# Seven-product groups and stored weight parts in the second half of a two-layer hybrid encoder

## The reference

```
for l in range(2):
    h = rmsnorm(x, norm_gain[l])
    q, k, v, g_attn, x_rnn, g_rnn = split(h @ w_in[l])       # 2048 x 4352
    attn = sliding window attention with sinks and rotary positions (16 heads, 2 kv heads, head size 64)
    rnn  = RG-LRU(causal width-4 conv(x_rnn)), run as a scan over the tokens
    x = x + concat(attn * silu(g_attn), rnn * silu(g_rnn)) @ w_out[l]   # 2048 x 2048
out = rmsnorm(x, final_gain)
```

## Time and profile before

| | |
|---|---|
| time, median of 3 runs | 2304.1 us (2302.57 to 2304.14) |
| time of the profiled execution | 2304.23 us |
| its span | 2301.7 us |
| PE busy | 2292.8 us, 100% of the span |
| DVE busy | 1565.0 us, 68% |
| ACT busy | 1339.1 us, 58% |
| granted clock of PE | 1.00 |
| DMA, mean over the span | 125 GB/s |

### The profile page before, as it was taken

One profiled execution on the slowest core, in us unless ns is written; L12 is line 12 of the kernel. 1 busy time (PEld: TensorE's weight loads), 2 busy tenths in 40 slices (PEclk: granted clock), 3 DMA queues, 4 the chain that ended last, 5 costly groups with the idle time before them and its releaser, 6 DMA issues.

```text
span 2301.7 us, 36298 instructions
## 1 busy us (share of the span) xinstructions
PE 2292.8 (100%) x13798; PEld 1919.3 (83%) x13798; DVE 1565.0 (68%) x2546; ACT 1339.1 (58%) x2564; POOL 32.3 (1%) x58
## 2 busy tenths in 40 slices
PE   9999999999999999999999999999999999999999
PEld 8877888899888888889888888888988888888898
DVE  7658868656646877856675786885565478778555
ACT  7557666445546857645564676763455557666444
POOL 1110000000000000000000000000000000000000
PEclk9999999999999999999999999999999999999999
DMA  8886334545333233344534333344543333333444
GB/s 259 237 243 174 88 92 120 152 138 139 96 93 98 86 89 92 96 145 139 163 110 152 111 95 89 96 139 138 142 131 96 97 91 86 93 92 96 117 136 152
DMA packets 141389, 287.48 MB, mean 125 GB/s; under 512 B 16416, under 2 KB 20768, under 8 KB 138784
## 3 DMA queue, kind: packets, MB, share of 16 engines
q1 hardware_dynamic: 138096, 259.91, 38.1%
q0 software_dynamic: 2688, 25.17, 4.5%
q10 hardware_dynamic: 432, 0.10, 0.0%
HBM read 276.73 MB, written 33.55 MB: 135 GB/s over the span
## 4 chain that ended last, share of the span: by engine, by line
PE 96%; DVE 2%; DMA 1%; ACT 1%; issue 0%; DVEq 0%; POOL 0%; ACTq 0%; POOLq 0%
PE proj L682 80%; PE proj L703 10%; PE ps_at L811 2%; DMA wall<-in_w 1%; PE ps_at L786 1%; PE ps_at L830 1%; PE proj L722 1%; ACT wcut L905 0%; DVE wcut L1307 0%; PE proj L749 0%; PE ps_at L640 0%; DVE mixed L1791 0%; DVE acc L1402 0%; ACT operand L942 0%; PE ps_at L764 0%
## 5 line engine op out<-in xcount | busy, mean ns | idle before, releaser
L682 PE MATMUL proj<-operand,wcut 128*128 128x512 f32 x8376 | 1944.0, 391 | 1.3 <-DVE xr L1558 1.3
L682 PEld LDWEIGHTS proj<-operand,wcut 128*128 128x128 f32 x8376 | 1563.7, 188 | 337.9 <-issue 10.3
L1307 DVE TENSOR_TENSOR wcut<-wall,wcut 128x512 fp32r<-128x512 f32 x871 | 600.1, 689 | 582.0 <-ACT wcut L905 575.1
L905 ACT ACTIVATE wcut<-wall 128x512 fp32r<-128x512 f32 x870 | 548.3, 630 | 547.2 <-DMA wall<-in_w 381.0
L703 PE MATMUL proj<-xsum_out,wcut 128*128 128x256 f32 x1104 | 136.8, 283 | 0.0
L703 PEld LDWEIGHTS proj<-xsum_out,wcut 128*128 128x128 f32 x1104 | 134.9, 192 | 0.6
L703 PEld LDWEIGHTS proj<-operand,wcut 128*128 128x128 f32 x828 | 105.3, 191 | 3.9 <-DVE proj L1371 0.3
L703 PE MATMUL proj<-operand,wcut 128*128 128x256 f32 x828 | 106.6, 283 | 0.0
L1011 ACT ACTIVATE gy<-proj 32x512 f32<-32x512 f32 x144 | 85.1, 591 | 26.6 <-PE proj L682 22.1
L1102 ACT ACTIVATE sqr<-ps_at,pars 64x512 f32<-64x512 f32 x64 | 43.9, 685 | 91.8 <-PE ps_at L830 91.4
L1063 ACT ACTIVATE prob<-ps_at,stat 128x128 f32<-128x128 f32 x256 | 90.1, 363 | 0.8
(11 more groups left out here) (173 smaller groups left out, 1520.6 us busy)
## 6 DMA issues: line engine op xcount, KB each, us to landing
wall<-in_w SPq DMA_DIRECT2D x710, 256.0 KB, 2.6
wall<-weight_sums SPq DMA_DIRECT2D x92, 256.0 KB, 2.7
weight_sums<-in_blocks POOLq DMA_DIRECT2D x36, 512.0 KB, 6.5
wall<-in_blocks SPq DMA_DIRECT2D x69, 256.0 KB, 2.6
x<-in_xt SPq DMA_DIRECT2D x16, 512.0 KB, 3.8
mixed<-in_xt SPq DMA_DIRECT2D x14, 512.0 KB, 6.7
weight_sums<-weight_sums POOLq DMA_DIRECT2D x12, 512.0 KB, 5.2
gw<-in_gates SPq DMA_DIRECT2D x32, 128.0 KB, 2.6
```

The costliest lines, as they stand in the source:

```text
L682: last = pe.matmul(bank_of(l, 2 * g + m)[:, :], wcut[:, n % RING, a, c:c + P], operand[:, k, b, :], start=(i == 0 and k == 0), stop=(k == ...
L905: act.activation(wcut[:, u % RING, 0, :], wall[:, u % RING, 1, :], ACT.Copy).then_inc(w_hi, 1)
L1307: dve.tensor_tensor(wcut[:, u % RING, 1, :], wall[:, u % RING, 1, :], wcut[:, u % RING, 0, :].bitcast(F32), ALU.subtract).then_inc(w_lo, 1)
```

## The change

The groups 7 to 16 of layer 1 and 4 to 16 of layer 2 of the in-projection are computed in seven products too, in the second half only. For it:

- the first half computes the same groups with eight full-width units, four of them on blocks (`beats_of`, kind "block"); after a unit's weights are split, both parts (512 KB) are stored to a new DRAM tensor `cuts`, for seven of the eight units of each group (`STORED`, 161 in all);
- the second half loads such a unit's two parts ready-made (`READY`, 161 units of 512 KB); ACT and DVE have no split to make for them, and PE waits for the load itself;
- the sums of blocks of these groups are built by POOL in 12 more batches, at times given by `OPENS`: five batches at once, four more from (half 1, layer 2) slot 1, six from (half 2, layer 1) slot 4, the last three from (half 2, layer 2) slot 1;
- in the second half `operand_sums` runs for the in-projection at the slots of `T_AT` (already in the code); its space is that of x, so in (half 2, layer 2) x is stored (4 MB, slots 1 to 4) and reloaded;
- in the second half a group's second query tile is moved out one slot after the first instead of four, and `rope` waits for the shifted copy before both of its multiplications;
- `IN_LAST` becomes 16, by which x is reloaded eight slots later.

```diff
-IN_LAST = 15
-IN_SEVEN = {(0, 0): (), (0, 1): (), (1, 0): (), (1, 1): ()}
+IN_LAST = 16
+IN_SEVEN = {(0, 0): (), (0, 1): (), (1, 0): range(7, IN_LAST + 1), (1, 1): range(4, IN_LAST + 1)}
...
-CUT_AT, READY, STORED = {}, set(), []
-SPLIT_NO = {n: n + 1 for n in range(TOTAL + UPG - RING)}
+KEYS = []
+CUT_AT = {}
+for n, (h, l, kind, g, j) in enumerate(UNIT):
+    if h == 0 and zone_of(g) == "in" and g in BUILT[l] and (kind, j) != ("block", WHOLE[A21]):
+        CUT_AT[key_of(l, kind, g, j)] = n
+        KEYS.append(key_of(l, kind, g, j))
+READY = {n for n, (h, l, *unit) in enumerate(UNIT) if h > 0 and key_of(l, *unit) in CUT_AT}
+STORED = sorted(CUT_AT.values())
+SPLIT = [n for n in range(TOTAL + UPG - RING) if n not in READY]
+SPLIT_NO = {n: i + 1 for i, n in enumerate(SPLIT)}
...
+def stores_through(n):
+
+    return sum(m % RING == n % RING for m in STORED if m <= n)
...
-Q_AT = [2 * UPG + 4 * t for t in range(AT)]
+Q_AT = [[2 * UPG + UPG * (t // 2) + (4, 1)[h] * (t % 2) for t in range(AT)] for h in range(HALVES)]
...
+OPENS = {5: (0, 1, 1), 9: (1, 0, 4), 15: (1, 1, 1)}
...
+                if n in READY:
+                    from_n = CUT_AT[key_of(l, kind, g, j)]
+                    sp_.wait_ge(cut_out[from_n % RING], 16 * stores_through(from_n))
+                    sp_.dma_start(wcut[:, n % RING, :, :].rearrange("p a c -> p (a c)").bitcast(F32),
+                                  cuts[KEYS.index(key_of(l, kind, g, j))]).then_inc(w_in[n % RING], 16)
+                    return
                 sp_.dma_start(wall[:, n % RING, 1, :], source(at)).then_inc(w_in[n % RING], 16)
...
                                 sp_.wait_ge(unit_done, u + 1)
+                                if u in STORED:
+                                    sp_.wait_ge(cut_out[u % RING], 16 * stores_through(u))
                                 w_load(u + RING)
+                            if u + 2 in STORED:
+
+                                sp_.wait_ge(w_lo, SPLIT_NO[u + 2])
+                                sp_.dma_start(cuts[KEYS.index(key_of(l, *UNIT[u + 2][2:]))],
+                                              wcut[:, (u + 2) % RING, :, :].rearrange("p a c -> p (a c)").bitcast(F32)
+                                              ).then_inc(cut_out[(u + 2) % RING], 16)
...
+                if n in OPENS:
+                    pool.wait_ge(built[S4], 32 * n - 16)
+                    add(S4, n - 1, A12)
+                    pool.wait_ge(unit_done, at_unit(*OPENS[n]))
...
-                if before:
+                if before and n not in OPENS:
...
-                pe.wait_ge(w_lo, SPLIT_NO[n])
+                if n in READY:
+                    pe.wait_ge(w_in[n % RING], 16 * (n // RING + 1))
+                else:
+                    pe.wait_ge(w_lo, SPLIT_NO[n])
...
             def rope(h, l, n, tile):
 
+                dve.wait_ge(shift_done, per_layer(h, l, 4 * (AT + 1), 4 * n + 4))
                 dve.tensor_tensor(gy[:, 0, :], bank_of(l, tile)[:, :], tab[:, 0, :], ALU.mult)
-
-                dve.wait_ge(shift_done, per_layer(h, l, 4 * (AT + 1), 4 * n + 4))
```

More of the change, by code:

```diff
@@ L294, in build @@
         x_kept = nc.dram_tensor("x_kept", (4, P, KT // 4 * TOK), F32).ap()
+        cuts = nc.dram_tensor("weight_cuts", (len(KEYS), P, 2 * KU * GW), F32).ap()
         rout = mu
@@ L320, in build @@
         built = {n: sem(f"built{n}") for n in SUMS}
+        cut_out = [sem(f"cut_out{i}") for i in range(RING)]
         kept = [sem(f"kept{i}") for i in range(4)]
@@ L1210, in _ @@
                             key_cross(h, l)
-                        if s in Q_AT:
-                            t = Q_AT.index(s)
+                        if s in Q_AT[h]:
+                            t = Q_AT[h].index(s)
                             shift(h, l, t + 1, tile_of("q", t))
@@ L1744, in _ @@
                         for t in range(AT):
-                            if s == Q_AT[t] + 1:
+                            if s == Q_AT[h][t] + 1:
                                 query(h, l, t)
```

## The result

| | before | changed |
|---|---|---|
| time, median | 2304.12 us (2302.57 to 2304.82, 4 runs) | 2330.1 us (2326.29 to 2333.69, 4 runs) |
| span of the profiled execution | 2301.7 us | 2328.5 us |
| PE busy | 2292.8 us | 2286.7 us |
| mean granted clock of PE | 1.000 | 0.995 |

The account below looks back on a forecast made before the run. The prediction took PE to bound the kernel: 2304.23 us, less 17.7 gained, plus 1 (queries), 0.5 (gates, inputs, `lead_sums`) and 2, 2, 1 (POOL's overlaps), gives 2293.0 us. Its range was 2286 to 2303 us.

Parts of the forecast that it names:

- What bounds the kernel: Whole kernel: PE, busy 2292.8 of 2301.7 us; only fewer PE units or PE waits can move the time.
- the gain: Second half: 23 groups turned into seven products save 0.77 us each, 17.7 us in all, the ceiling.
- POOL's overlaps: Four places where POOL's batches run beside new stores or loads, (A) to (D): 0, 2, 2 and 1 us.
- (B): First half, layer 2: batches 5 to 8 beside stores from near 652 us; 2 us lost (0 to 8).
- (C): Second half, layer 1: six batches beside ready-made loads from near 1285 us; 2 us lost (0 to 8).
- (D): Second half, layer 2: x stored in slots 1 to 4 beside three batches; 1 us lost (0 to 6).
- (A): Start of the run: batches 0 to 4 end near 175 us, stores begin near 163; 12 us of overlap, hidden.
- the query tiles: Second half: second tile out after 8.3 of 11.0 us, in time except the last query group; 1 us lost.
- The last pair of layer 2: Second half, layer 2, slots 40 to 42: exponents and normalisation queue ahead, late by 0 to 2 us; 1 taken.
- gates, inputs and `lead_sums`: New groups of the second half: small margins before PE needs them; 0.5 us lost (0 to 5).
- the second rival: Late evacuation: PE waits for DVE in every new group, gain gone, 2304 us (band 2299.7 to 2308.7); chance 0.11.
- The third rival: Stores and loads don't fit the DMA, SP falls behind in every stored group: 2333 us; chance 0.10.

Follow-up runs that it names:

- e9: Changed kernel with ten new groups in each layer, old query slots, POOL's batches apart from stores, last layer's x stored and summed later: 2290.96 us, ratio 0.995.
- e2: Changed kernel with the same eighteen POOL batches started elsewhere, mostly beside out-projection groups: 2339.92 us, ratio 1.0163.
- e3: Changed kernel with only the last three POOL batches moved, to (half 2, layer 1) slot 144: 2329.93 us, ratio 1.0101.
- e1: Changed kernel without POOL's twelve new batches, in-projection groups reading out-projection sums instead: 2313.85 us, ratio 1.0046.
- e12: e9 with the five batches of (half 1, layer 2) begun at slot 54, where stores begin, instead of slot 1: 2338.1 us, ratio 1.0151.
- e5: Changed kernel with POOL's copies and adds cut into pieces of 2 KB instead of 32 KB and 8 KB: 2341.81 us, ratio 1.0162.
- e6: Changed kernel with the query tiles of (half 2, layer 1) back at their old slots: 2321.98 us, ratio 1.0085.
- e8: Changed kernel with POOL's pieces of 2 KB and old query slots in (half 2, layer 1) and for layer 2's first pair: 2327.61 us, ratio 1.0107.

## Why the prediction was wrong

**What bounds the kernel** and **the gain** were right: 23 groups in seven products give 20.7 us, I had 17.7. The pace of 21.00 us holds where no attention runs; where scores and values run a new group gains some 0.95 us instead of the 0.77 I took, which I have not explained.

**Failed: POOL's overlaps were under-sized, 5 us for 28.** The places (B), (C), (D) were named, and (A) was rightly nothing. B: predicted 2 (0 to 8), measured 10.4. C: 2 (0 to 8), measured 3.2 beside the output stores and 6.2 beside the ready-made loads. D: 1 (0 to 6), measured 8.2. The sum of shares of 1.33, 16 us of work too much, pointed the right way. The error was to call 10 us of it hidden and to discount the rest by the row in which PE lost only 1.6 us from 28 to 204 us: there SP asked for a share of 0.3 and the sum stayed under 1.

I also read the parts' beginnings 8 us too soon from the earlier trace rows: the first matmul of (half 1, layer 2) starts at 578.8 us in the kernel before, that of (half 2, layer 1) at 1148.5. That left B's overlap as long as I had it; at C POOL worked from 1174 to some 1363 us and ready-made loads began at 1307.5, 55 us of overlap instead of 40.

The runs give a price for each place. Beside plain loads (shares 0.33 + 0.56) a batch costs 0 to 0.3 us (before, e9). Beside seven-product groups of the out-projection (0.49 + 0.56) it costs 1.4 to 3 us (e2, e3), which the shorter time of six units may explain as well. Beside stores (0.73 + 0.56) it costs 5 to 9 us (changed kernel, e1, e12).

That POOL would keep its share when SP asks for more I had as the consequence of a rule of the Trainium skill ("DMA: Bandwidth & Descriptors", Queues, rings and completion order). At the full queue of e12 the trace agrees with that consequence, 52.6%. That the size of the packets is the reason is not shown: in e5 POOL kept 53.4% with pieces of 2 KB, at queues not quite full. I gave it 8 us at B; the chain of the changed kernel shows why it is more, a store landing late, then the load that had to wait for it on SP:

```profile
672.02 14.02 DMA weight_cuts<-wcut
...
686.11 4.95 DMA wall<-in_blocks
...
691.15 0.64 ACT wcut L942
...
694.62 9.47 DMA weight_cuts<-wcut
...
706.19 10.05 DMA wall<-in_w
...
722.19 3.02 PE proj L719 x12
```

I had allowed a store 4 us and 10 us of lateness to be hidden once. The two on the chain took 14.0 and 9.5, and SP's wait for a store delays everything behind it: 32.6 us of such waits between 655 and 720 us, the longest 8.0. By itself such a wait costs nothing: e9 has 111.5 us of them in the whole run, none over 2.8.

**Failed: the query tiles, 1 us for 18.** I worked out when the second tile is out of its bank (8.3 us), and asked only whether that is in time for PE. I did not name what is queued behind ACT's wait, which is the weight splits that PE needs next. ACT (waits in brackets), then PE, around slot 41 of (half 2, layer 1):

```profile
1282.94 0.64 ACT L942 ACTIVATE wcut<-wall 128x512 fp32r<-128x512 f32 x1
1290.12 2.43 ACT L1048 ACTIVATE gy<-proj 32x512 f32<-32x512 f32 x4 [6.54 <-DVE q L1532]
...
1293.96 0.64 ACT L942 ACTIVATE wcut<-wall 128x512 fp32r<-128x512 f32 x1
```
```profile
1294.14 1.98 PE L823 MATMUL ps_at<-kboth,q 64*64 64x128 f32 x32 [5.03 <-ACT prob L1100]
1296.05 4.35 PE L719 MATMUL proj<-operand,wcut 128*128 128x512 f32 x12
1301.78 13.89 PE L719 MATMUL proj<-operand,wcut 128*128 128x512 f32 x60 [1.37 <-DVE wcut L1344]
```

Eleven microseconds pass between two splits, with a new unit due every 2.72. DVE's query stands behind a weight split that waits for ACT, and behind an operand sum; ACT's next shift waits for that query. And in layer 1, where the first new group is 7, nobody needs those banks sooner; e6, e8 and e9 do without. The last pair of layer 2, which I priced at 1 us (0 to 2), held PE for 2.88 us and the next unit at half clock. What slots 8 to 48 of that layer lose without POOL, lead units and gain taken out (11.4 - 5.8 + 1.7), is some 7 us. I put it down to the queries; of the changed kernel's own layer 2 only the first pair was tested (2.2 us, e5 against e8).

**Missing: the clock.** I had a price for idle PE, none for what comes after it. The twelve wide matmuls after the 5.03 us wait took 4.35 us, where twelve at the end of the chain above took 3.02. The mean granted clock fell from 1.000 to 0.995. Before its last matmul the changed kernel has four stretches at half clock, 1.2 GHz instead of 2.4; these are the two longest:

```profile
701.58:708.41 6.83, 5.49 (x12) 3.80 (x12) 1.36 (x2) 6.63 (x21) 0.77 (x1) 0.50 0.77 252
1292.09:1298.91 6.82, 4.77 (x39) 3.86 (x40) 3.74 (x6) 6.59 (x16) 1.98 (x4) 0.50 0.69 235
```

The four last 20.5 us, and PE is busy for 16.8 of them; at full clock that work would take half, so I estimate 8 of the 47 us. They are contained in the losses above.

**Missing: group 16 of the first half, 1.6 us.** Its blocks read odd tiles of `operand` two slots later than plain units did, and `mixed_hi` on ACT, which overwrites them, waits with weight splits behind it: 0.8 us in each layer, in every run that has these blocks.

**Right:** gates, inputs and `lead_sums` in the new groups (0.5 us taken, nothing seen where POOL is silent), so the second rival is out: the groups gain 0.8 to 0.95 us each. (Its band was also half a microsecond off: 2304.2 - 17.7 + 23 x 0.55 or 0.95 is 2299.1 to 2308.3.) The third rival, stores and loads that don't fit, is out as well: without POOL a stored group keeps its pace at a share of 0.73 and 240 GB/s. No rival had the cause; the third, 2333 us, had only the size. The sum of the terms in the changed kernel: -20.7 + 28 + 18 + 1.6 + 0.7 (reloads) = 27.6 us against 26.6 measured at the last slots.

## What to carry to other kernels

Add the DMA shares of everything that runs in a stretch, by queue; where the sum passes 1, price it in full and take no comfort from a stretch where the sum was below 1. Ask too how long the loads ahead last there: six units were 16.3 us of plain work and 11.5 of narrow. When a step is moved forward on an in-order engine, ask not only whether it ends in time but what stands behind the wait that it brings. And place transfers with no deadline where the other queue is light: the same batches cost 47 us or nothing, by when they began.

## What the runs showed of the hardware

POOL's DRAM-to-DRAM queue did not yield: 56% of the DMA engines beside plain loads, 53% with them full (e12). Its 2 KB pieces held nearly the share of pieces four to sixteen times as large for a fifth fewer bytes. In the changed kernel PE waits of 2.8, 2.9, 3.0 and 5.0 us came with matmuls at half clock, 20.5 us of it in all, while one of 2.7 us did not. So such a wait costs more than its length: some 8 us on top of the 33 us of idle PE that the change added. e9 has no stretch at half clock before its last matmul.
